# Gates, convolution and head norms of a hybrid layer moved into the attention stages beside them; two orders of work changed

## The reference

```python
h = rms_norm(x, norm_g) * (1 + scale) + shift                  # the same for the context
aq, ak, av, az, bq, bk, bv, bo, bz, bg, cq, ck, cv, cz, gm = split_proj(h @ w_in)
# a: differential attention, 4 heads of 128
y_a = rms_norm(o_a, da_g) * (1 - lam_init) * silu(az)          # norm over each head
# b: bidirectional gated recurrence, computed here as a 768 x 768 attention with decays
qk = silu(conv3(concat(bq, bk)) + conv_b)                      # depthwise, over tokens
log_i, log_f = gates(bg) ; log_f = log_sigmoid(log_f)          # 16 gate values a token
h_b = mlstm_forward(...) + flip(mlstm_backward(...))           # cumulated log_f, running maximum
y_b = sigmoid(bo) * rms_norm(h_b, ml_g) * silu(bz)             # norm over each head
# c: neighbourhood attention
y_c = o_c * silu(cz)
x = x + gate * (sum_n sigmoid(gm_n) * (y_n @ w_br[n])) @ w_out
# the A/B layer: a gated linear recurrence and a retention side by side
xr = causal_conv4(xr); lru = scan(a(xr), u(xr)) * gelu(y)
ret = groupnorm(retention(rotary(q), rotary(k), v)) * silu(g)
```

## Time and profile before

| what | value |
|---|---|
| median of three runs | 3790.86 us (3790.77 to 3798.38) |
| the profiled execution's own time | 3798.5 us |
| its span | 3796.8 us |
| mean granted TensorE clock | 0.943 of full |
| TensorE busy | 3361.2 us (89%) |
| VectorE busy | 1786.1 us (47%) |
| ScalarE busy | 1280.9 us (34%) |
| GpSimd busy | 64.4 us (2%) |
| transfers | 263.06 MB, mean 69 GB/s |

### The profile page before, as it was taken

The page is one execution under the profiler, slowest core; times in us unless marked ns, Lnnn a source line. Parts: engine busy times, 40 slices in busy tenths (PEclk is TensorE's granted clock), DMA queues, the critical chain, the costliest instruction groups (busy, mean ns, idle before and its releaser), DMA issues. The chain is left out here.

```text
span 3796.8 us, 47171 instructions
## 1 busy us (share of the span) xinstructions
PE 3361.2 (89%) x19416; PEld 1880.5 (50%) x19416; DVE 1786.1 (47%) x2681; ACT 1280.9 (34%) x2034; POOL 64.4 (2%) x116
## 2 busy tenths in 40 slices
PE   6999788889999799869799978789998988889998
PEld 3566545656655366626555434334443455544443
DVE  4234466655633435456566444743333246644332
ACT  2224343334422214344344333233222125533321
POOL 0000001100000000001000000000000000000000
PEclk9999999999999899989899989899999978899999
DMA  6311010021122211110211312122223200012222
GB/s 265 142 48 45 16 46 31 13 81 43 46 94 73 74 57 56 37 57 28 60 59 65 131 69 78 56 78 89 100 95 114 78 34 1 1 56 89 100 91 76
DMA packets 47253, 263.06 MB, mean 69 GB/s; under 512 B 5656, under 2 KB 7320, under 8 KB 26432
## 3 DMA queue, kind: packets, MB, share of 16 engines
q1 hardware_dynamic: 46464, 256.89, 19.4%
q10 hardware_dynamic: 576, 3.15, 0.2%
HBM read 253.62 MB, written 4.19 MB: 68 GB/s over the span
## 5 line engine op out<-in xcount | busy, mean ns | idle before, releaser
L357 PE MATMUL banks<-h_sb,wsplit_sb 128*128 128x512 f16 (+2 forms) x7872 | 1624.4, 361 | 118.2 <-PEq L77 38.7
L357 PEld LDWEIGHTS banks<-h_sb,wsplit_sb 128*128 128x128 f16 x7872 | 762.1, 99 | 903.1 <-issue 238.5
L343 DVE SCALAR_TENSOR_TENSOR wsplit_sb<-ring_sb,wsplit_sb 128x2048 f16<-128x2048 f32 (+2 forms) x214 | 443.5, 2073 | 486.3 <-ACT wsplit_sb L334 485.4
L357 PE MATMUL banks<-quads,wsplit_sb 128*128 128x512 f16 (+1 forms) x2880 | 603.5, 366 | 19.3 <-issue 10.3
L334 ACT ACTIVATE wsplit_sb<-ring_sb 128x2048 f16<-128x2048 f32 (+2 forms) x214 | 370.8, 1733 | 734.0 <-PE banks L357 683.4
L357 PEld LDWEIGHTS banks<-quads,wsplit_sb 128*128 128x128 f16 x2880 | 281.7, 99 | 320.6 <-issue 53.7
L357 PE MATMUL banks<-wsplit_sb,h_sb 128*128 128x256 f16 x2112 | 250.6, 274 | 0.0
L462 ACT ACTIVATE quads<-banks 128x512 f32<-128x512 f32 (+2 forms) x230 | 109.6, 479 | 348.4 <-PE banks L357 347.9
L357 PEld LDWEIGHTS banks<-wsplit_sb,h_sb 128*128 128x128 f16 x2112 | 205.4, 98 | 39.8 <-issue 13.0
L545 PE MATMUL banks<-quads 64*128 64x256 f32 (+3 forms) x432 | 114.1, 517 | 7.4 <-PEq L77 7.4
L568 PE MATMUL banks<-work_sb,quads 128*128 128x128 f32 x832 | 106.7, 276 | 1.6 <-ACT work_sb L600 1.6
(11 more groups left out here) (328 smaller groups left out, 3222.5 us busy)
## 6 DMA issues: line engine op xcount, KB each, us to landing
ring_sb<-in_w_in SPq DMA_DIRECT2D x52, 1024.0 KB, 4.8
ring_sb<-in_w_ffn SPq DMA_DIRECT2D x44, 1024.0 KB, 4.7
ring_sb<-in_w_merge SPq DMA_DIRECT2D x48, 768.0 KB, 4.1
ring_sb<-in_w_ffn SPq DMA_DIRECT2D x32, 704.0 KB, 4.0
quads<-in_w_mod SPq DMA_DIRECT2D x12, 1024.0 KB, 25.8
x_sb<-in_w_mod SPq DMA_DIRECT2D x12, 1024.0 KB, 4.9
ring_sb<-in_w_ab SPq DMA_DIRECT2D x12, 1024.0 KB, 4.8
ring_sb<-in_w_nsa SPq DMA_DIRECT2D x10, 1024.0 KB, 4.9
```

Of the source, the lines that this page charges most:

```text
L343: dve.scalar_tensor_tensor(m.wsplit[:, g % 2, 1, 0:n], m.ring[:, g % 2, 0:n], WSCALE, m.wsplit[:, g % 2, 0, 0:n], ALU.mult, ALU.subtract). ...
L357: mm = pe.matmul(p.bank, *p.terms(k, pw, px), start=(p.opens and k == 0 and z == 0), stop=(p.closes and k == p.depth - 1 and z == 2))
```

## The change

`head_norm` and `gates_window` are gone as stages. A class `HeadNorm` holds the same operations as streams with planned times; `mlstm_window` weaves a's norm into its front, `neighbour_window` b's norm. Scores of their own attentions wait until the norm's products are there, since they share scratch and banks; in both the attention's units are planned to start later (26 and 27 instead of 8 and 2), while dense parts fill the front. The gate products become two parts of 384 columns in `diff_window`, with the cumulative sums, the convolution and the transposes beside the softmax. The SiLUs and sigmoids become tanh with multiplications by VectorE: `silu(x) = 0.5 x (1 + tanh(x/2))`, with the halves moved into constants. Dense groups 16 to 19 move into the recurrence's stage.

```diff
-def head_norm(nc, m, name, y, gain, gates, ntok):            # whole stage removed
-    with stage(nc, *(f"{name}_{q}" for q in ("sel", "sq", "sum", "rec", "root", "wide", "steps", "hi", "lo"))) as (
...
+class HeadNorm:
+    def squares(self, act):
+        for h in range(KB):
+            yield self.t0 + h
+            act.activation(self.sq[h][:, 0:self.ntok], self.y[:, h, 0:self.ntok], ACT.Square).then_inc(self.squared, 1)
+        yield self.t0 + 13.0
+        act.wait_ge(self.steps, 2 * len(self.chunks))
+        act.activation(self.rstd, self.rstd, ACT.Sqrt).then_inc(self.rooted, 1)
+    def sums(self, pe):
+        for h in range(KB):
+            yield self.t0 + 1.3 + 1.3 * h
...
+    def inverse(self, dve):
+            yield self.t0 + 7.0 + 4.0 * i
...
+    def spread(self, pe):
+            yield self.t0 + 14.0 + 3.0 * h
...
+    def scale(self, dve):
+            yield self.t0 + 15.5 + 3.0 * h
+            dve.wait_ge(self.widened, h + 1)
+            step(dve.scalar_tensor_tensor(t, self.y[:, h, 0:self.ntok], self.gain, self.banks(h + 1)[:, 0:self.ntok],
+                                          ALU.mult, ALU.mult))
+            dve.tensor_tensor(t, t, self.gates[:, h, 0:self.ntok], ALU.mult).then_inc(self.product, 1)
...
 def diff_window(nc, m, l, wt, with_ctx):
+            if i == 0:
+                for a, b in chunks_of(T):
+                    terms = lambda kk, pw, px, a=a, b=b: (gates16[:, pw, kk, :], part(m.h, px, kk, a, b))
...
+                    parts.append(Part(8, b - a, KD, terms, "act", store, before=(gate_lo, 1), rows=16))
...
+        parts.append(Part(13, 96, 0, None, "act", column_store, before=(gsteps, 13), emit=gate_columns, cost=2.6))
...
+                                      lambda act, p, o=o: act.activation(o, p, ACT.Tanh, scale=0.5 * UNSCALE)))
...
+            conv_at.append(max([last_part[i].t1 + 1.5] + [t + 9.0 for t in conv_at[-1:]]))
...
+                act.activation(m.tmp[:, i % 2, 0:n], m.tiles[:, 16 + i, 0:n], ACT.Tanh, scale=0.5).then_inc(tanh_done, 1)
...
+                dve.scalar_tensor_tensor(x, m.tmp[:, i % 2, 0:n], 1.0, x, ALU.add, ALU.mult).then_inc(activated, 1)
...
-            weave(*a.vector(dve), d.split_lo(dve), d.stores(dve, "dve"))
+            weave(*a.vector(dve), gate_dve(dve), conv_dve(dve), conv_end(dve), d.split_lo(dve), d.stores(dve, "dve"))
...
 def mlstm_window(nc, m, l, wt, with_ctx):
+        norm = HeadNorm(m, nsems, 2.0, m.tiles[:, 0:KB], m.da_gain[:, l:l + 1], m.tiles[:, 12:16], ntok,
+                        [m.tiles[:, 8 + i, :] for i in range(KB)])
...
-        d = Dense(m, wt, parts, (6, 7), dsems, extra=4.0 * len(units))
-        a = Attention(m, units, asems, 8.0, d.span / (len(units) + 2.0), (.6, 0, .2, .5, 1.05, 1.55, 1.75, 2.05, 2.25),
+        d = Dense(m, wt, parts, (6, 7), dsems, extra=4.0 * len(units) + 10.0)
+        start = 26.0
+        a = Attention(m, units, asems, start, (d.span - start + 6.0) / (len(units) + 2.0),
...
+        a.after_norm = (norm.product, KB)
...
 def neighbour_window(nc, m, l, wt, with_ctx):
+        norm = HeadNorm(m, sems[18:], 2.0, m.tiles[:, 16:20], vec(m, "ml_g", l), m.tiles[:, 28:32], ntok,
+                        [m.tiles[:, 20 + i, :] for i in range(KB)])
...
+        start = 27.0
+        unit_us = (d.span - start - 2.0) / (sum(weight) + 2.0)
...
 def opening(nc, m, l, wt, qchunks):
-        parts[3].pause = 4 * pair - sum(p.cost for p in parts[0:4]) if start else 6.0
+        parts[3].pause = 18.4 - sum(p.cost for p in parts[0:4]) if start else 6.0
-        at = (lambda k: pair * (k // 2) + 0.5 * pair * (k % 2)) if start else (lambda k: 1.9 * k)
+        at = lambda k: 2.3 * k if start else 1.9 * k
-        row_at = lambda n: 0.5 * pair * n - pair if n < 8 else 28.0 + later * (n - 8)
+        row_at = lambda n: 2.4 * n - 20.0 if n < 8 else 28.0 + later * (n - 8)
...
     opening(nc, m, l, wt, qchunks)
     diff_window(nc, m, l, wt, with_ctx)
-    head_norm(nc, m, "dn", m.tiles[:, 0:KB], m.da_gain[:, l:l + 1], m.tiles[:, 12:16], ntok)
-    gates_window(nc, m, l, wt, with_ctx)
     mlstm_window(nc, m, l, wt, with_ctx)
-    head_norm(nc, m, "mn", m.tiles[:, 16:20], vec(m, "ml_g", l), m.tiles[:, 28:32], ntok)
     neighbour_window(nc, m, l, wt, with_ctx)
...
-AB_ORDER = (4, 6, 8, 2, 3, 9, 5, 7, 10, 11, 0, 1)
+AB_ORDER = (2, 3, 4, 6, 8, 9, 5, 7, 10, 11, 0, 1)
```

487 lines of the change are left out of this document (250 added, 237 removed).

## The result

The changed kernel took 3678.8 us (median of 4 runs, 3670.9 to 3680.2) against 3790.9 us before: a ratio of 0.9695, 95% interval 0.968 to 0.971, so 112 us faster where 150 were forecast. The profiled execution took 3679.3 us with a span of 3677.6. Against the span of before, 3796.8 us, that is 119 us; the profiled execution of before was itself 7.5 us above its median, so 7 of the 119 us belong to that one execution and not to the change.

The account below looks back on a forecast made before the run. TensorE, busy 89% of the span, leaves gaps in norms, gates and the VectorE-paced recurrence. Layer 0 -73, layer 1 -61, opening -6, A/B -10 make -150: 3790.9 to 3641 us; own range 3618 to 3666, stated range 3600 to 3690.

Parts of the forecast that it names:

- rival 2: Opening and A/B stage: both reorderings lose, opening +3, A/B +15 instead of -16 us; 3675 us, chance 0.14.
- The recurrence: Merged recurrence windows: dense products fill VectorE waits; 238 and 199 us, with 11 and 10 allowed for front, end, leftover waits.
- The merge of the norms: Head norms inside recurrence and third attention: TensorE work counted at full clock, 11.0 us in layer 0, 8.5 in layer 1.
- what stands between the unit's first small step and its reciprocal ... costs little: First attention, VectorE's queue: steps placed there fall into the time of ScalarE's exponentials and cost little.
- 9 us of new waits on layer 0 and 6 on layer 1: First attentions: added TensorE waiting from VectorE's extra work, within windows of 236 and 185 us.
- the 2 for the norm's front: Third attentions: 2 us allowed for the merged head norm's front, besides 11.0 and 8.5 us of TensorE work.
- and the first product to 47: Opening of layer 0: first dense product starts about 47 us, last step at 71, 8 us earlier; 6 us gain taken.
- the bound of +3: Opening of layer 0: upper bound, 3 us slower if the modulation rows come later than thought; lower bound -12.
- A/B stage: Recurrence input projected first puts recurrences beside dense products; about -10 us, near 259 us, bounds +15 and -25.
- The difference counts for both: Whole kernel: the -150 us applies alike to the profiled execution (3798.5 us) and the median (3790.9 us).
- rival 1: First attentions: VectorE takes the bound, every added microsecond (50 and 45) lands on the softmax chain; 3721 us, chance 0.11.
- Rival 4: First attention and recurrence: each of 80 units pays a lap of VectorE's and ScalarE's queues; 3817 us, chance 0.02.

Follow-up runs that it names:

- the run with dealt-out steps: Changed kernel with the first attentions' added VectorE steps spread in limited slots, convolution's tanh behind a unit's exponentials: 3648.1 us, ratio 0.9612.
- the best kernel: Changed kernel with VectorE steps spread evenly in the first attentions, later position table loads and the opening of before: 3633.5 us, ratio 0.9577.

## Why the prediction was right, and where it was not

The 3678.8 us lie in the stated range of 3600 to 3690, but above the 3618 to 3666 that the prediction calls the forecast's own. They stand next to rival 2's 3675, and rival 2 is not what happened: it had the A/B stage lose, which gained 11 us. So the range held by its width. What was right is the mechanism of the gain, merged windows that fill TensorE's gaps; the sizes fell short by 38 us, in the places below.

- **The recurrence** is right: 239.3 and 193.6 us against 238 and 199. Dense products filled what the VectorE-paced units left open, the wait for VectorE fell from 21.2 to 13.5 us (the prediction's sign was under 10). In layer 1 TensorE's work was 185.0 us where 189 was forecast, and 8.6 of the allowed 10 us were used; in the ten other profiles with the same stage it took 190.4 to 191.9 us with some 182 us of work.
- **The merge of the norms** was priced by TensorE's 15.3 us at 0.72 becoming 11 at full clock. The window gave back 15.4 and 14.3 us in layer 0: 3 to 4 us more each than its product time. With 121 us of stages gone this was the safe part of the gain.
- **First attention**, "what stands between the unit's first small step and its reciprocal ... costs little": this step failed, for want of a limit. Up to about 1.9 us at that place did cost little (the run with dealt-out steps). The changed kernel has 4.6 us there in one unit of layer 0 and 6.3, a weight split among them, in one of layer 1, and TensorE waited 5.61 and 3.23 us behind them. Nor is that place better than the other: the run with all steps behind the weights was as fast in layer 0. The term "9 us of new waits on layer 0 and 6 on layer 1" was mis-sized: 10.9 and 13.0 us more waiting for L1020 alone. Beside it the forecast took TensorE's work as 201.1 + 9.5 us, at full clock; it was 218.3, at a granted clock of 0.95 (the prediction's sign was 0.96 or more). With the steps dealt out it was 212.4 us at 0.98 (211.9 in the best kernel), and the windows 228.8 and 181.4 us, under the forecast's 236 and 185. The forecast's size can be had with an even spread; the changed kernel has an uneven one.
- **Third attention**, "the 2 for the norm's front": too small. In layer 1 8.4 of its 15.2 us more are one wait for a root behind a late weight transfer. The forecast did not read SyncE's queue in this stage. The kernel before issued the tables ahead of the weights too (at 1880.02, for 7.62 us), but the root then had a stage of its own and stood behind no split. In layer 0 the two waits around the norm are 2.4 us for the root and 1.6 for the first product of VectorE behind it (L947), 4 us where 2 were counted.
- **Opening**, "and the first product to 47": the start was wrong by 9.5 us (56.50). The column product at 40.49 waited 3.51 us for VectorE's gains, which stood behind a reciprocal of 3.35 us. The last three rows then start 3.4 and 4.0 us apart (41.40, 44.78, 48.80) and take 1.93 us each instead of 1.07, at the lower clock. Behind the last column (51.23) gains, scale, high and low half come one after another, and TensorE waits 4.26 us for them. The beat behind the start is right: from 56.50, with two steps in the first row, to 81.09 for the eighth are 3.4 us each for all but one. The stage lost 5 us in this profile, about 4 over all of them, where the forecast had a gain of 6; the bound of +3 did not hold it.
- **A/B stage**: right in size and in mechanism, -11.2 against -10, with the two large waits going from 12.6 and 6.1 to 2.2 and 4.8 us.
- **"The difference counts for both"** (profiled execution and median): wrong by 7 us. The stage of sparse attention alone, which the change doesn't touch, took 272.1 us in one profile and 269.6 in the other. Differences between two profiles carry a few us that the medians don't: 2.5 us in this stage, 7 in the whole.
- The rivals: a piece of rival 1 came true (19 of its 80 us) and a piece of rival 2 (the opening, not A/B). Rival 4, the lap of both queues in every unit, is seen in 3 of the 24 units of the first attention of layer 0, where a tanh delays the exponentials by 1.3 us, and in none of the 16 of layer 1.

## What to carry to other kernels

When side work joins a window whose units run in a fixed order, count it per unit and not per window: the same VectorE steps made the two windows 29 and 24 us longer in heaps and 12 and 12 us longer dealt out, little more than the 9.5 us (an estimate from the earlier trace rows) of TensorE work that came with them. When a stage is merged, read also the queue that issues transfers: what stood there harmlessly for a stage may now stand ahead of something that is needed at once. And of a change in several parts, undo each singly: here the shortest edit (an order of twelve numbers) brought 13 us, the longest 30, and one part lost 4.

## What the runs showed of the hardware

In the first attention of layer 0 more waiting and a lower granted clock (a mean between the two levels of 1.2 and 2.4 GHz) came together. Six profiled executions with the steps in heaps waited 24.7 to 27.5 us for L1020 at a clock of 0.94 to 0.96, with 216.5 to 219.1 us busy. The five with the steps dealt out or without the convolution waited 12.0 to 13.3 us at 0.98 or 0.99, with 209.5 to 212.4 us busy. The products are the same, so that is 4 to 10 us on top of the waiting. That the waiting lowers the clock is not shown, and layer 1 speaks against so simple a rule: the changed kernel's code ran once with TensorE busy 175.7 us at 0.99, waiting 15.0 us, in 193.6 us, and in five other kernels with the same code in this window 183 to 184 us at 0.94, waiting 10.2 to 10.6 us, in 196.8 to 197.2 us. So 8 us more of busy time made the window only 3 us longer; 5 us of it took the place of waiting for VectorE. The recurrence behind it was shorter in those (190.7 us against 193.6 where its code was the same), so the two stages together differ by less than 1 us. A window's length is steadier than either number, and it is what should be compared.
